# Stage joints of a two-block transformer kernel, worked in halves

## What is computed

```python
x = x + 0.5 * swiglu_ffn(rmsnorm(x, g1), w_gu1, w_down1)
x = x + mixer(rmsnorm(x, g), ...)          # ab, nsa; then even, odd
x = x + 0.5 * swiglu_ffn(rmsnorm(x, g2), w_gu2, w_down2)
x = x + gate * (p[i] @ ple_w_in[i])        # second block only; gate = sigmoid(rms_norm(x) @ w_gate)
```

## Time and profile before

| | |
|---|---|
| time, median of 3 runs | 2478.39 us (2478.05 to 2479.03) |
| the profiled execution | 2476.12 us, span 2474.3 us |
| PE busy | 2291.2 us, 93% of the span, 12236 products |
| DVE / ACT / POOL busy | 68% / 51% / 9% |
| HBM read | 359.76 MB, 146 GB/s over the span |

### The profile page before, as it was taken

One profiled execution on the slowest core, in us unless ns is written; L12 is line 12 of the kernel. 1 busy time (PEld: TensorE's weight loads), 2 busy tenths in 40 slices (PEclk: granted clock), 3 DMA queues, 4 the chain that ended last, 5 costly groups with the idle time before them and its releaser, 6 DMA issues.

```text
span 2474.3 us, 33426 instructions
## 1 busy us (share of the span) xinstructions
PE 2291.2 (93%) x12236; PEld 1915.2 (77%) x12236; DVE 1688.1 (68%) x2930; ACT 1270.3 (51%) x2052; POOL 211.5 (9%) x125
## 2 busy tenths in 40 slices
PE   7998869999998999899899896989999999879998
PEld 6887858888887955788788775767886888767886
DVE  7875877778774444777877647537776877567775
ACT  5654645555552334555555554416555555246553
POOL 0003310000002200000000114200001000210001
PEclk9999979999999857999999997879999999889999
DMA  6542344445543400455455232005553554215452
GB/s 264 203 171 106 120 145 170 180 178 189 195 164 128 140 26 26 145 180 194 154 195 190 102 139 94 1 30 183 187 187 141 196 192 145 103 60 195 180 196 73
DMA packets 64366, 362.98 MB, mean 147 GB/s; under 512 B 7433, under 2 KB 8201, under 8 KB 32201
## 3 DMA queue, kind: packets, MB, share of 16 engines
q1 hardware_dynamic: 63776, 360.31, 40.3%
q10 hardware_dynamic: 296, 0.27, 0.0%
q0 software_dynamic: 128, 0.26, 0.0%
HBM read 359.76 MB, written 1.05 MB: 146 GB/s over the span
## 4 chain that ended last, share of the span: by engine, by line
PE 79%; DVE 13%; ACT 5%; issue 1%; DMA 1%; DVEq 0%; POOL 0%; ACTq 0%; SPq 0%
PE ps L188 78%; DVE work L129 3%; DVE WL L118 3%; ACT work L178 3%; DVE work L118 2%; PE ps L193 2%; ACT WH L178 2%; ACT XBt L178 1%; DVE Xt L129 1%; DVE small L129 1%; DMA ring<-wts 1%; DVE HLt L118 1%; DVE small L141 1%; DVE XBt L129 0%; DVE work L125 0%
## 5 line engine op out<-in xcount | busy, mean ns | idle before, releaser
L188 PE MATMUL ps<-XBt,WH 128*128 128x512 f32 (+1 forms) x3936 | 1216.9, 370 | 43.7 <-DVE WL L118 22.7
L118 DVE TENSOR_TENSOR WL<-ring,WH 128x1024 fp32r<-128x1024 f32 x603 | 746.5, 1238 | 289.1 <-ACT WH L178 258.8
L188 PE MATMUL ps<-XBt,WL 128*128 128x256 f32 x3376 | 896.6, 283 | 0.0
L178 ACT ACTIVATE WH<-ring 128x1024 fp32r<-128x1024 f32 x662 | 702.0, 1060 | 327.8 <-PE ps L188 267.8
L188 PEld LDWEIGHTS ps<-XBt,WH 128*128 128x128 f32 x3936 | 706.0, 193 | 152.8 <-DVE XBt L129 19.9
L188 PEld LDWEIGHTS ps<-XBt,WL 128*128 128x128 f32 x3376 | 648.9, 192 | 30.6
L178 ACT ACTIVATE work<-ps 128x256 f32<-128x256 f32 (+5 forms) x511 | 212.3, 415 | 473.9 <-PE ps L188 446.1
L118 POOL TENSOR_TENSOR WL<-ring,WH 128x1024 fp32r<-128x1024 f32 x59 | 144.7, 2452 | 1687.0 <-ACT WH L178 1686.7
L188 PE MATMUL ps<-WH,HHt 128*128 128x512 f32 x704 | 276.7, 393 | 10.7 <-DVE HLt L118 10.3
L188 PE MATMUL ps<-WL,HHt 128*128 128x512 f32 x704 | 274.4, 390 | 0.0
L188 PE MATMUL ps<-WH,HLt 128*128 128x512 f32 x704 | 274.3, 390 | 0.0
(11 more groups left out here) (105 smaller groups left out, 1357.9 us busy)
## 6 DMA issues: line engine op xcount, KB each, us to landing
ring<-wts SPq DMA_DIRECT2D x248, 1024.0 KB, 5.8
ring<-wts SPq DMA_DIRECT2D x180, 512.0 KB, 3.8
ring<-wts SPq DMA_DIRECT2D x1, 1152.0 KB, 5.3
ct<-cons SPq DMA_DIRECT2D x1, 1086.5 KB, 12.3
Xt<-x SPq DMA_DIRECT2D x2, 512.0 KB, 4.7
out<-Xt SPq DMA_DIRECT2D x1, 1024.0 KB, 4.1
ring<-wts SPq DMA_DIRECT2D x2, 256.0 KB, 2.8
ring<-wts SPq DMA_DIRECT2D x1, 288.0 KB, 2.8
```

The lines of the kernel that those rows point to most:

```text
L118: self.done(self.e and self.e.tensor_tensor(out, a, b, op), inc)
L178: self.done(self.e and self.e.activation(out, a, f, **kw), inc)
L188: inst = self.e and self.e.matmul(out, l, r, start=start, stop=stop)
```

## The change

- An FFN's end: the last down products are ordered by column half n; the last H, HH and HL are made per token tile; POOL starts on the next stage's splits only after the last HL.
- `follow`: a stage whose norm is `unscaled` hands its first half (transposes of the columns of n=0, and the first flip on DVE) to the stage before, which runs it as soon as `x00` and `x10` are there, ahead of its last products on PE and ahead of `x01` and `x11` on DVE.
- The first product group of the next stage (`head`) starts with kt 0 and 1, then the transposes of the second half, then the rest.
- ACT: flips of half 0, two Squares of 512 columns, the copy of the FFN's piece 0 part 2, flips of half 1, two Squares. DVE adds the two sums of squares.
- In an FFN the row product moves from behind the products of piece 0 into the middle of the gate product of piece 1.
- At a mixer's end only parts 0 and 1 of the next piece 0 are copied and split; the copies of piece 1 move behind the last Square.
- For every FFN but f1.0, POOL splits part 2 of piece 0 and parts 0 and 1 of piece 1.
- x is loaded in four transfers for two; fin writes x in four parts.

The diff, cut to its core. All mixers call `last_pe`, `last_act`, `last_dve`; nsa and od give `norm` as `head` to their first `cm_pe`, ple to its first `tms_pe`, and call `norm.dve(V, q)` for q from 1 to 4, with a split of their second piece's part 0 after q=3; ab and ev make what is missing of their first two pieces behind their norm. The function `product` makes the gate or up products of the given kt as before.

```diff
         def on_pool(name, part):
+            if COLS[name] == 3072 and name[0] in "fg":
+                t, j = name.rsplit(".", 1)
+                return t != "f1.0" and (j, part) in (("0", 2), ("1", 0), ("1", 1))
             return part == 1 and COLS[name] == 2048 and name not in ROPE
...
+        def cm_pe(P, piece, t, head=None):
...
+            for kts in (range(2), range(2, 4), range(4, 8)) if head else (range(8),):
+                for u in range(2):
+                    P.wait_ge(f"{piece}:lo{u}")
...
+                if head and kts[0] == 0:
+                    head.pe(P, 1)
             ps.give(piece, f"{piece}.e")
...
+        def last_pe(P, t):
+            for n in range(2):
+                for i in range(2):
+                    if n and i and t in follow:
+                        follow[t].pe(P, 0)
+                    out_pe(P, t, 1, n, i)
...
                 for i in range(2):
                     xv = X[:, i, n * 512:n * 512 + 512]
                     V.wait_ge(f"{t}_w{n}.1" + ("" if i else ":i0"))
                     V.tt(xv, ps[f"{t}.w{n}{i}"], xv, ADD, inc=f"{t}.x{i}{n}")
-                lo(V, ahead(f"{t}_w{n}.1"))
...
-        def out_act(A, t):
-            for n in range(2):
-                hi(A, ahead(f"{t}_w{n}.1"))
-
-        def out_pool(G, t):
-            for n in range(2):
-                lo(G, ahead(f"{t}_w{n}.1"))
...
+                if n == 0:
+                    lo(V, ahead(f"{t}_w0.1"), (0, 1))
+                    if t in follow:
+                        follow[t].dve(V, 0)
+        def last_act(A, t):
+            hi(A, ahead(f"{t}_w0.1"), (0, 1))
...
+            SQ4 = work[:, 2048:4096].rearrange("p (n i d) -> p n i d", n=2, i=2)
+            def pe(P, half):
+                flip_pe(P, t, X, half, lambda i, half: f"{prev}.x{i}{half}")
+            def act(A, between=None):
+                flip_act(A, t, g, 0)
+                for half in range(2):
+                    for i in range(2):
+                        A.wait_ge(f"{prev}.x{i}{half}")
+                        A.act(SQ4[:, half, i, :], X[:, i, half * 512:half * 512 + 512], ACT.Square,
+                              accum_out=n_s4[:, 2 * half + i:2 * half + i + 1], inc=f"{t}.sq" if half and i else None)
+                    if not half and between:
+                        between(A)
+                    if not half:
+                        flip_act(A, t, g, 1)
+            def dve(V, q):
+                if q < 4:
+                    flip_dve(V, t, g, q)
+                else:
+                    V.wait_ge(f"{t}.sq")
+                    V.tt(n_ss, n_s4[:, 0:2], n_s4[:, 2:4], ADD)
+                    scale_dve(V, t)
+                    for i in range(2) if rows else ():
+                        V.ts(DG[:, hs(i)], IDN, n_r[:, i:i + 1], None, MUL, None, inc=f"{t}.dg" if i else None, back=1 + i)
+            follow[prev] = Stage(pe, act, dve, (lambda G: flip_pool(G, t)) if whole else None)
+            return follow[prev]
...
+            def down_last(P, n):
+                j, piece = NFF - 1, last
+                wh, wl = wide(piece)
+                ws = slice(2048 + n * 512, 2560 + n * 512)
+                P.wait_ge(f"{piece}:lo2")
+                for i in range(2):
+                    P.wait_ge(f"{t}.hh{j}{i}")
+                    P.mm(ps[f"{t}.acc{i}{n}"], HH[:, j % 2, hs(i)], wh[:, ws], False, False)
+                    P.mm(ps[f"{t}.acc{i}{n}"], HH[:, j % 2, hs(i)], wl[:, ws], False, False)
+                for i in range(2):
+                    P.wait_ge(f"{t}.hl{j}{i}")
+                    P.mm(ps[f"{t}.acc{i}{n}"], HL[:, j % 2, hs(i)], wh[:, ws], False, True,
+                         inc=f"{piece}:d" if n and i else f"{t}.fin{i}{n}")
...
             def pe(P):
-                norm.pe(P)
-                for i in range(2):
-                    for n in range(2):
-                        ps.take(f"{t}.acc{i}{n}")
+                if first:
+                    norm.pe(P, 0)
...
+                    for kts in (range(2), range(2, 4), range(4, 6), range(6, 8)) if j == 0 else (range(8),):
+                        for u in range(2):
+                            P.wait_ge(f"{t}.{j}:lo{u}", *ps.free(f"{t}.{'gu'[u]}{j}"))
+                            if j == 1 and u == 0:
+                                product(P, j, u, range(4))
+                                row_pe(P, t)
+                                product(P, j, u, range(4, 8))
+                            else:
+                                product(P, j, u, kts)
+                        if j == 0 and kts[0] == 0:
+                            norm.pe(P, 1)
+                    for u in range(2):
+                        ps.give(f"{t}.{'gu'[u]}{j}", f"{t}.{'gu'[u]}{j}.e")
                     if j == 0:
-                        row_pe(P, t)
-                    else:
-                        down(P, j - 1)
-                down(P, NFF - 1)
-                for i in range(2):
-                    for n in range(2):
-                        ps.give(f"{t}.acc{i}{n}", f"{t}.x{i}{n}")
+                        for use in ("acc00", "acc10", "acc01"):
+                            ps.take(f"{t}.{use}")
+                    if j == 1:
+                        ps.take(f"{t}.acc11")
+                    if 0 < j < NFF - 1:
+                        for n in range(2):
+                            for i in range(2):
+                                down(P, j - 1, n, i)
+                for n, i in ((0, 0), (0, 1), (1, 0)):
+                    down(P, NFF - 2, n, i)
+                down_last(P, 0)
+                down(P, NFF - 2, 1, 1)
+                for i in range(2):
+                    ps.give(f"{t}.acc{i}0", f"{t}.x{i}0")
+                if t in follow:
+                    follow[t].pe(P, 0)
+                down_last(P, 1)
+                for i in range(2):
+                    ps.give(f"{t}.acc{i}1", f"{t}.x{i}1")
...
             def act(A):
-                norm.act(A)
-                hi(A, f"{t}.0")
+                hi(A, f"{t}.0", (0, 1))
+                norm.act(A, lambda A: hi(A, f"{t}.0"))
+                hi(A, f"{t}.1", (0, 1))
...
-                    hi(A, nx2, (0,))
+                    if j < NFF - 1:
+                        hi(A, nx2, (0,))
                     A.wait_ge(f"{t}.gm{j}")
                     A.act(TH[:, b, :], GU[:, b, 0:256], ACT.Tanh, scale=0.5, inc=f"{t}.th{j}")
+                    hi(A, nx2, (0,))
...
+                    if j < NFF - 1:
...
+                    else:
+                        A.act(LW[:, b, 256:512], ps[f"{t}.u{j}"][:, 256:512], ACT.Copy, inc=f"{t}.ul{j}")
+                        for i in range(2):
+                            A.wait_ge(f"{t}.h{j}{i}", f"{t}.{j - 2}:d")
+                            A.act(HH[:, b, hs(i)], H[:, b, hs(i)], ACT.Copy, inc=f"{t}.hh{j}{i}")
+                        hi(A, nx2, (1,))
...
             def dve(V):
-                norm.dve(V)
-                lo(V, f"{t}.0")
+                lo(V, f"{t}.0", (0, 1))
+                for q in range(0 if first else 1, 5):
+                    norm.dve(V, q)
+                    if q == 3:
+                        lo(V, f"{t}.1", (0,))
                 for j in range(NFF):
...
-                    lo(V, nx1, (0, 1))
+                    if j:
+                        lo(V, nx1, (0, 1))
                     V.wait_ge(f"{t}.gl{j}")
                     V.tt(GU[:, b, 0:256], ps[f"{t}.g{j}"][:, 0:256], LW[:, b, 0:256], ADD, inc=f"{t}.g{j}.e")
                     if j == 0:
+                        lo(V, nx1, (1,))
                         row_dve(V, t)
                     V.tt(GU[:, b, 0:256], GU[:, b, 0:256], RB, MUL, inc=f"{t}.gm{j}")
-                    lo(V, nx2, (0,))
+                    if 0 < j < NFF - 1:
+                        lo(V, nx2, (0,))
+                    if j == 0:
+                        lo(V, f"{t}.0")
                     V.wait_ge(f"{t}.th{j}")
...
+                        lo(V, nx2, (0, 1) if j else (0,))
+                        V.wait_ge(f"{t}.hh{j}")
+                        V.tt(HL[:, b, :], H[:, b, :], HH[:, b, :].bitcast(F32), SUB, inc=f"{t}.hl{j}")
+                        lo(V, nx2, (0, 1))
+                        lo(V, nx1, (2,))
+                        if first:
+                            params_dve(V, j)
+                V.ts(n_q, n_r, 0.25, None, MUL, None)
+                j, b = NFF - 1, 1
+                for i in range(2):
+                    us = slice(256 + i * 128, 384 + i * 128)
...
+                    V.tt(GU[:, b, us], ps[f"{t}.u{j}"][:, hs(i)], LW[:, b, us], ADD, inc=f"{t}.u{j}.e" if i else None)
+                    V.tt(H[:, b, hs(i)], SG[:, b, hs(i)], GU[:, b, us], MUL, inc=f"{t}.h{j}{i}")
+                for i in range(2):
+                    V.wait_ge(f"{t}.hh{j}{i}")
+                    V.tt(HL[:, b, hs(i)], H[:, b, hs(i)], HH[:, b, hs(i)].bitcast(F32), SUB, inc=f"{t}.hl{j}{i}")
+                for n in range(2):
+                    for i in range(2):
```

(56 more changed lines are left out.)

236 lines of the change are left out of this document (95 added, 141 removed).

## The result

| | before | after |
|---|---|---|
| time, median of 4 runs each | 2478.71 us (2478.05 to 2480.76) | 2498.90 us (2498.21 to 2499.22) |
| ratio to before | | 1.008, 95% interval 1.0062 to 1.0097 |
| the profiled execution's span | 2474.3 us | 2496.4 us |

The forecast was 2485, with 2455 to 2492 as the range. The direction and the mechanism of the likeliest case were right, the size was not: the time lies above the range, where case D had been given 1 in 10.

A forecast was written before the change was run, and what follows sets the result against it. PE, busy 93% of the span, was taken as the bound. The terms summed to +6.65 us: 2482.8 from the profiled execution's 2476.12, or 2485 on the median of 2478.39; range 2455 to 2492.

The forecast's parts named there:

- the likeliest case: Joints into five FFNs: all three POOL splits starve DVE's chain; 2478 to 2491 us, chance 0.55.
- case D: Late splits also hold back the next piece's copies and ring slots, or the start loses too: over 2491 us, chance 0.10.
- HL (-1.2): End of f1.0, into ab: POOL's split waits for DVE's last HL, net -1.2 us (bounds -1.7 and -0.4).
- FFN to FFN (-1.45): f2.0 into f1.1: first down product 20.75 us after the last gate/up product, before 22.2, so -1.45.
- Mixer to FFN (+10.0): Four joints: DVE's chain held by POOL's splits, then lower clock; +3.0 at ab and od, +2.0 at nsa and ev.
- rival B: Mixer-to-FFN joints: POOL blocks DVE's chain once only, no clock lost; sum -29, 2449 us, chance 0.17.
- ple: g2.0 and g2.1 into ple: gates start earlier, -6.0 us (bounds -3 and -6.5); ple to g1.1: +4.5.
- nsa and od (+1.0): FFN into nsa and od: row product 0.4 us earlier, but PE's longer pause costs clock; +0.5 each.
- Start (0): Start of f1.0: product 0 ends some 2 us earlier, first down product stays at 29.7; 0, bounds -2 and +1.
- fin and g1.0 (-0.5): f2.1, fin, g1.0: x in four parts starts flips early, x01 and x11 wait on DVE; -0.5 (bounds -2 and +0.5).
- g1.0 to ev (+0.3): g1.0 into ev: the copy of ev_q part 2 moves behind the flips; +0.3 us (bounds 0 and +1.3).

The follow-up runs named there:

- e4: The kernel before, with POOL's splits at the end of each FFN made to wait for DVE's last HL: 2468.30 us, ratio 0.9959.
- e3: The changed kernel with POOL's three splits at the start of f2.0, f2.1, g2.0, g1.1 and g2.1 waiting for `dg`, the end of DVE's chain: 2490.23 us, 1.0049.
- e5: The changed kernel with no FFN split on POOL; DVE does them, that of piece 1 part 0 behind its chain: 2489.45 us, 1.0047.
- e7: The changed kernel with ACT copying piece 1 part 0 in place of piece 0 part 2, and POOL waiting for `dg` behind its first split: 2488.63 us, 1.0043.
- e6: The changed kernel with POOL's last two sums XF of nsa and od waiting for `dg`: 2484.75 us, 1.0028.
- e8: The changed kernel with x in two loads and ACT's flips early again, piece 0's copies and splits right behind the flips: 2491.80 us, 1.0061.
- e10: e9 with all 16 transposes and all flips ahead of g1.0's first product, x still in four parts: 2459.49 us, 0.9932.
- e9: The changed kernel with e8's start, e6's wait, a modified e7 joint at f2.0, f2.1, g2.0, g2.1, and g1.1's splits on DVE: 2463.15 us, 0.994.
- e11: e9 with DVE's split of piece 0 part 2 moved from between two pairs of flips at f2.0, f2.1, g2.0 and g2.1: 2453.57 us, 0.9894.

## Why the prediction was wrong, step by step

- **HL (-1.2): right.** -1.44 measured; e4 shows 1.6 to 1.8 for each end by itself.
- **FFN to FFN (-1.45): right.** f1.1's first down product comes 15.03 behind f2.0's last one, for 17.08; f2.0 itself is 0.93 longer, since eight transposes now stand ahead of its last products. -1.12 in all.
- **Mixer to FFN (+10.0): the mechanism right, the size too large.** +5.5 measured. The pause at the row product was put at 4.9 and is 3.80 (one instruction more got past each split than counted), and the lower clock lasts 2.9 us (0.50 over 381.1 to 384), not over the whole 4.2 that follow. e3 shows that the blocking is the cause of that pause. Once nothing blocks the chain the joint in halves is worth 0.9 to 3.1 us against the kernel before in e5 and 2.8 to 4.0 in e7: rival B's picture, which the code as written never reaches.
- **ple: half right.** The end of the kernel gains 1.46 for 3.1: PE now waits 1.10 and 0.31 for DVE's splits inside ple, the lower bound that the step named. pl0 and g1.1 together were +1.6 and are +1.66.
- **nsa and od (+1.0): the step that failed most, +8.9 measured.** It counted XF and DVE's split, and not that ACT's copy of the next piece lets POOL begin another split just as DG is due: 2.1 us. The pause became 4.98, the row product came 1.4 us (nsa) and 1.1 us (od) later where 0.4 earlier was forecast, and the clock term was whole, 2.5 for the 0.9 taken. Removing both collisions (e6) gives 3.2 us per place back, and the clock some of the time. The +5.1 of od also holds 1.5 from the later part of its middle (64.64 for 63.12), which other executions of untouched code show too (65.48 in e4), so this part cannot be charged to the change.
- **Start (0): failed, +7.25.** The step put the copies of piece 0 ahead of ACT's flips at no cost, and gave no time at which piece 0 lands. It lands at 10.7 (9.3 to 9.4 in four kernels with the same start), later than the 8.2 with two loads of x; ACT's table load (1.28) is paid only then, where before it ran at 5.52; and the transposes of the second half stand behind the first products. The step weighed DVE's queue (it bounds HL in e8, as it said) and not ACT's. With the order and the loads undone the product is back at 29.68 (e8).
- **fin and g1.0 (-0.5): wrong by 2.3.** The sum had x01 and x11 as the loss; the trace shows the first products in the slow stretch. Open in part, see e10.
- **g1.0 to ev (+0.3): inside its bounds** of 0 to 1.3, with 1.04; no run looks at it by itself.

One reading of the prediction was off without a bearing on the sum: the chain holds four tensor_scalar, not five.

The Trainium skill's page "SBUF — State Buffer", section "Who interferes with whom", says that the order of issue and not the kind of instruction decides which of VectorE and GpSimd is blocked. e9 and e11 agree: with POOL 0.13 us ahead DVE's split takes 3.33 and POOL's 2.39, with DVE 0.84 ahead they take 1.23 and 2.63.

## What to carry to other kernels

When work moves onto a second engine, look at what the first engine does in those microseconds: fourteen tiny DVE instructions on the critical path are the worst neighbours of long POOL instructions (9.0 us for 2.85 here), and one wait that puts the long ones behind the chain, or in front of it, decides whether the move pays. Ask of every queue, the first one at the start above all, what its first instruction waits for. A pause of PE has two prices, its length and the clock of what follows it. The second belongs in the sum in full where the rows show it nearly every time (3.4 us and more here), and as a range below that.

## What the hardware showed

- The clock behind a pause of PE, read at the row products of nsa and od in thirteen kernels, over the next 5 us: behind 1.0 to 1.2 us it is 1.00 in all four cases; behind 1.8 it is 1.00 in four and 0.66 in four; behind 4.8 to 5.0 it is 0.50 to 0.69 in all fourteen. Pauses of 3.4 to 3.9 us anywhere in the thirteen traces, where the clock was 1.00 for the 3 us ahead of them, are followed by a lower mean in 54 cases of 55. Near 1.8 us the length of the pause does not decide it. Executions of one code differ by it: in od, with a pause of 1.8 in both, e11 takes 47.38 us from the row product to the next long gap and e9 44.05 (clock 0.66 and 1.00 in the first 5 us).
- A small DVE instruction with its inputs in SBUF stands until the POOL split beside it is over; in the ab joint one more then passes before the next one is held, though POOL's splits follow each other within 0.15 us (2.40 for two, 2.29 for one, 2.38 for two).
- With x in four transfers of 256 KB the first 14 us moved 308 to 313 GB/s in six kernels, with two of 512 KB 341 to 347 in seven. A part of it is that the weights' loads are issued 0.94 us later. Between 4 and 8 us the rate is lower too, 293 to 356 GB/s against 389 to 422 in windows of 2 us.
